# Attention's value products issued once per pair of heads, the first head's one step later

## The reference

```
sc = einsum('bhqd,bhkd->bhqk', qi, k) * scale      # + decay terms for the fox heads
sc = where(kpos <= qpos, sc, -inf)
p  = softmax(sc, axis=-1)
o  = einsum('bhqk,bhkd->bhqd', p, v)               # the value product
```

## Time and profile before

| | us |
|---|---|
| median of 3 runs | 959.61 |
| lowest and highest of them | 958.34 and 964.16 |
| the profiled execution, its own time | 958.37 |
| its span in the trace | 956.5 |

### The profile page before, as it was taken

The page is one execution under the profiler, slowest core; times in us unless marked ns, Lnnn a source line. Parts: engine busy times, 40 slices in busy tenths (PEclk is TensorE's granted clock), DMA queues, the critical chain, the costliest instruction groups (busy, mean ns, idle before and its releaser), DMA issues.

```text
span 956.5 us, 13462 instructions
## 1 busy us (share of the span) xinstructions
PE 927.1 (97%) x5645; PEld 815.0 (85%) x5645; DVE 680.6 (71%) x784; ACT 497.0 (52%) x629; POOL 56.4 (6%) x79
## 2 busy tenths in 40 slices
PE   8999999999999999989999999999899999999997
PEld 7999878888888799976688888887899898888886
DVE  4976895897896865566758975668677866566664
ACT  5646854544636565666544545555354544444442
POOL 2025002000000000010010000000000000000000
PEclk9999999999999999999999999999999999999999
DMA  9743278899895462223579976655555455665531
GB/s 299 233 134 133 93 265 287 282 349 333 283 308 179 132 221 72 89 89 132 167 283 341 323 270 201 217 179 174 173 183 182 150 183 191 194 199 176 183 126 45
DMA packets 122756, 192.54 MB, mean 201 GB/s; under 512 B 6630, under 2 KB 103176, under 8 KB 119496
## 3 DMA queue, kind: packets, MB, share of 16 engines
q1 hardware_dynamic: 116496, 157.00, 50.2%
q0 software_dynamic: 5824, 33.90, 9.7%
q10 hardware_dynamic: 376, 0.78, 0.2%
HBM read 190.60 MB, written 1.06 MB: 200 GB/s over the span
## 4 chain that ended last, share of the span: by engine, by line
PE 71%; DVE 8%; ACT 4%; issue 2%; DVEq 0%
PE PS L663 19%; PE PS L664 10%; PE PS L615 9%; PE PS L617 9%; PE PS L616 9%; PE PS L608 3%; PE PS L610 3%; PE PS L609 3%; DVE lo L1698 3%; ACT hi L1230 1%; DVE stats L1784 1%; PE PS L736 1%; DVE r L1777 1%; DVE x_tok L1797 1%; ACT hid L1559 1%
## 5 line engine op out<-in xcount | busy, mean ns | idle before, releaser
L1698 DVE TENSOR_TENSOR lo<-raw,hi 128x2048 fp32r<-128x2048 f32 (+1 forms) x147 | 329.5, 2264 | 94.3 <-ACT hi L1230 94.2
L663 PE MATMUL PS<-x_both,hi 128*128 128x512 f32 x848 | 297.0, 393 | 0.0
L1230 ACT ACTIVATE hi<-raw 128x2048 fp32r<-128x2048 f32 (+1 forms) x147 | 271.7, 1885 | 9.1 <-DMA raw<-even_w_in 5.1
L664 PE MATMUL PS<-x_both,lo 128*128 128x256 f32 x848 | 237.5, 280 | 0.0
L663 PEld LDWEIGHTS PS<-x_both,hi 128*128 128x128 f32 x848 | 159.0, 187 | 35.7
L664 PEld LDWEIGHTS PS<-x_both,lo 128*128 128x128 f32 x848 | 159.9, 189 | 1.3
L615 PE MATMUL PS<-hi,hid_hi 128*128 128x512 f32 x352 | 139.3, 396 | 0.5 <-DVE hid_lo L1997 0.5
L617 PE MATMUL PS<-hi,hid_lo 128*128 128x512 f32 x352 | 138.9, 394 | 0.0
L616 PE MATMUL PS<-lo,hid_hi 128*128 128x512 f32 x352 | 138.8, 394 | 0.0
L608 PE MATMUL PS<-x_both,hi 128*128 128x256 f32 (+1 forms) x472 | 135.0, 286 | 3.0 <-DVE lo L1698 1.7
L609 PE MATMUL PS<-x_both,hi 128*128 128x256 f32 (+1 forms) x472 | 133.3, 282 | 0.0
(11 more groups left out here) (302 smaller groups left out, 1002.7 us busy)
## 6 DMA issues: line engine op xcount, KB each, us to landing
raw<-ffn_w_gate SPq DMA_DIRECT2D x22, 1024.0 KB, 7.8
raw<-ffn_w_up SPq DMA_DIRECT2D x22, 1024.0 KB, 6.3
raw<-ffn_w_down SPq DMA_DIRECT2D x22, 1024.0 KB, 5.1
raw<-mlp_w_in SPq DMA_DIRECT2D x16, 1024.0 KB, 5.3
raw<-mlp_w_out SPq DMA_DIRECT2D x16, 1024.0 KB, 5.0
sq<-ada_w POOLq DMA_DIRECT2D x12, 1024.0 KB, 7.1
r<-ada_w POOLq DMA_DIRECT2D x12, 1024.0 KB, 5.9
raw<-sc_w_in SPq DMA_DIRECT2D x12, 1024.0 KB, 5.2
```

The costliest lines, as they stand in the source:

```text
L663: pe.matmul(PS[:, bank + m, :], wh, x_both[:, :, k, :], start=k == 0, stop=False, skip_group_check=True)
L664: last = pe.matmul(PS[:, bank + m, 0:S], wl, x_hi[:, k, :], start=False, stop=k == KT - 1, skip_group_check=True)
L1230: act.activation(split_view("hi", c), split_view("raw", c), ACT.Copy).then_inc(hi_split, 1)
L1698: dve.tensor_tensor(split_view("lo", c), split_view("raw", c), split_view("hi", c).bitcast(F32), ALU.subtract).then_inc(lo_split, 1)
```

## The change

Only PE's program changes. `attend` now takes a pair of heads. It is called at even steps from 4 on, so the odd head's value product stays at its step, and the even head's moves from the odd step before to this one. The four products of the pair are written head by head for the first key block and then head by head for the second. The wait for `prob_t_ready` now asks for both heads, the wait for `o_lo` stands ahead of the pair, and `attended` still counts once for each head.

```diff
-            def attend(a):
-                pe.wait_ge(sem("prob_t_ready"), a + 1)
-                pair, e = a // 2, a % 2
-                if e == 0 and pair >= 1:
+            def attend(pair):
+                pe.wait_ge(sem("prob_t_ready"), 2 * pair + 2)
+                if pair >= 1:
                     pe.wait_ge(sem("o_lo"), pair)
-                if a in (0, FOX_H):
-                    pe.wait_ge(sem("odd_evac"), 18 if a else 2)
-                v, h = (v_tok, a) if a < FOX_H else (vm_tok, a - FOX_H)
-                pt = prob_t[:, a % 2, :]
-                pe.matmul(PS[64 * e:64 * e + 64, 3, 0:S], v[:, 0, h * 64:h * 64 + 64], pt[:, 0:S], start=True, stop=False,
-                          skip_group_check=True)
-                pe.matmul(PS[64 * e:64 * e + 64, 3, P:S], v[:, 1, h * 64:h * 64 + 64], pt[:, S:384], start=False, stop=True,
-                          skip_group_check=True).then_inc(sem("attended"), 1)
+                if pair in (0, FOX_H // 2):
+                    pe.wait_ge(sem("odd_evac"), 18 if pair else 2)
+                v, h = (v_tok, 2 * pair) if pair < FOX_H // 2 else (vm_tok, 2 * pair - FOX_H)
+                for j, qs, ks in ((0, slice(0, S), slice(0, S)), (1, slice(P, S), slice(S, 384))):
+                    for e in range(2):
+                        last = pe.matmul(PS[64 * e:64 * e + 64, 3, qs], v[:, j, (h + e) * 64:(h + e) * 64 + 64], prob_t[:, e, ks],
+                                         start=j == 0, stop=j == 1, skip_group_check=True)
+                        if j:
+                            last.then_inc(sem("attended"), 1)
...
-                if a >= 3:
-                    attend(a - 3)
+                if a >= 4 and a % 2 == 0:
+                    attend(a // 2 - 2)
```

## The result

The median after is 962.53 us of 10 executions (960.26 to 968.98), against 960.25 us (957.22 to 965.17) for the kernel before on the same chip: ratio 1.0039, 95% interval 1.0020 to 1.0058. By the ratio the change costs some 3.7 us (1.9 to 5.6); the two medians differ by 2.3. The forecast was 959.1, the range ended at 961.5, and the time lies above it, though within the 1% that was called no change.

The account below looks back on a forecast made before the run. PE bounds the whole kernel (97% busy), but ACT and DVE often bound the changed stretch. A gain of 1.5 us, less 0.3 and 0.65 given back, left -0.55 us: median 959.61 becomes 959.1, range 956.8 to 961.5.

Parts of the forecast that it names:

- Steps 3 and 4: Early attention: PE waits for DVE anyway up to 411.81, so the PE time saved there buys nothing.
- step 5: Attention, where head 2's product and its 1.63 us wait leave: `uq` 1 starts 3.07 us sooner, shift only -1.5 us.
- the wait before step 8: PE idle ahead of that step's scores, which wait for ACT: grows from 1.08 to 3.3 us.
- What a pair costs: Two heads' value products on PE: 0.92 us against 1.78 apart; seven pairs can gain 0.86 each, 6.0 us of PE.
- Rival 2: The two heads of a pair don't overlap on PE in this order: +1.4 us, 961.0; chance 0.05.
- term of 0.64: Extra us per pair if its heads don't overlap, counted three times on the chain: -0.55 + 3 x 0.64 = +1.4.
- Rival 3: ACT and DVE have more slack in steps 5 to 15, so PE's savings pass through: about 957.0 us; chance 0.10.
- steps 10 and 16: ACT's copies of heads 8 and 14 wait for the pair behind the transposes: 0.3 and 0.65 us given back.
- The shift is -1.2 us from there: From ACT's copy of head 8, starting at 442.6 instead of 443.83, carried through the later steps.
- rival 1: PE's clock falls in the longer wait, half speed for 3 us takes 1.5: +0.65 us, 960.3; chance 0.33.
- the shift stays: After the attention, PE's long feed-forward work has nothing of the change in it, so -0.55 us reaches the end.
- steps 16 to 18: End of the attention, no cover left: the copy waits for the pair, 0.65 given back, leaving -0.55 us.

Follow-up runs that it names:

- before_again: The kernel before, unchanged, run again for a second trace: 958.49 us, ratio 0.9995.
- four_buffers_warm: The changed kernel with four buffers for transposed probabilities instead of two, plus idle PE products where PE waits: 957.04 us, ratio 0.9983.
- pairs_warm_short: The changed kernel with idle PE products, each group sized a little under the PE wait it fills: 958.89 us, ratio 0.9994.
- warm_tail: The changed kernel with idle PE products only at the end of the attention: 959.55 us, ratio 1.0006.
- tail_single: The changed kernel with one pair undone, heads 12 and 13 issued apart as before: 958.51 us, ratio 1.0002.
- pairs_again: The changed kernel, unchanged, run again for a second trace: 964.18 us, ratio 1.0053.

## Why the prediction was wrong

**The steps before step 8: right against the profiled execution.** Steps 3 and 4 bought nothing; step 5 gave 1.58 for 1.5; the wait before step 8 was 3.29 for 3.3. Against `before_again` step 5 gives 0.16 (its mask of step 6 comes 3.75 after that of step 5, after's 3.59): see the base below.

**What a pair costs: right.** Six of after's eight pairs read 0.87 us for eight records, for 0.90, and the two that lie in a fall read 1.55. Rival 2 (no overlap) and its +1.4 are out. (Its term of 0.64 is not worked out; from the prediction's own rows it would be 2 x 0.80 + 0.09 - 0.92 = 0.77.) Rival 3 is out for this kernel, since A with the clock held came out at the forecast's shift; but what it says of slack is in part true: once the copy's wait is gone (`four_buffers_warm`), 2.13 of shift reaches L615, not 1.5. This also decides the weighing of the Trainium skill (TensorE: Matmul & The Clock Gate, The mechanism): under strict program order, read pass by pass as the prediction reads it, the pair would have cost 0.12 more, and the trace disagrees in the changed order too.

**Where ACT's wait for the pair leaves the chain at steps 10 and 16: right** with the clock held, -1.35, -0.51 and -0.55 in `pairs_warm_short`. What the wait takes was sized too low, 0.95 against 1.6; it didn't show because the transposes stood further ahead than the -1.5 that it was taken from.

**Failed: "The shift is -1.2 us from there", and with it rival 1's price.** Rival 1 had the mechanism and the first place: the clock fell behind the 3.3 us wait, the copy of head 8 shifted -0.23, near rival 1's 0. It was given 0.33 and should have been the forecast: the row that spoke against a fall has 1.78 us of idle time, and the earlier trace rows a fall behind 1.53 and 1.63, both shorter than the wait of 3.3 that was worked out.

**Failed: "the shift stays" after step 18.** Neither forecast nor rival asked what the price at the end does to PE's own waits. PE waits 1.41, 0.72, 0.58 and 0.97 us there in after (0.28, none, 0.55 and 0.93 in the earlier trace rows). The 1.41 is the place that head 12's product left; the 0.72 is the copy that starts later, and with four buffers it is gone. In both traces of after the clock falls there and stays at 0.50 for 10.2 us. Against `pairs_warm_short`, which met the forecast in these steps, this is 1.05 us within steps 16 to 18, from the copy of head 14 (1.1 late, the price of step 8's fall) to L615 (2.16 late), and 2.52 in the output product, a place that isn't in the change. That this place carries most of the loss is what `warm_tail` and `tail_single` show: with it filled or undone alone the ratio is 1.0006 and 1.0002, with intervals that hold 1.

**Failed: the base.** -0.55 was taken against an execution that held a fall of 1.45 us at step 5. The view stood in the prediction, as an argument for rival 1, and the sum didn't use it: the part of the -1.5 us that came from PE at half speed belongs to that execution, not to the order. Against an execution without it the order costs +0.9 us with the clock held. With both falls the traces give 51.20 - 48.15 = 3.05 in A and 2.52 in B, 5.6 us, or 4.1 against the profiled execution before. The medians differ by 2.3 in the first comparison and 4.9 in `pairs_again`'s: not every execution of after has both falls, and not every one of before is without.

**The range** ended at 961.5 since rival 1 was sized as one fall that returns what had been won. The runs show a price that isn't bounded so: in after it went on into 5.9 us of output product that the change doesn't touch.

**What stays open.** Why a fall comes in one execution and not in the next: at step 5 of before in one trace of two, and in after, where 6 of 22 executions have a mean clock of 0.992 or more. At an equal mean clock of 0.996 after's four executions (960.26 to 961.76) lie about 2.2 us above the kernel before's mean of 958.98, of which the order explains 0.9. The other 1.3 may be where the low windows lie, which the mean doesn't tell, or chance: the kernel before's 25 executions at 0.996 run from 957.28 to 964.15. No run tested it. That the wait itself, and not something else in the changed steps, makes the clock fall is shown only through idle products that fill it; both go together.

## What to carry to other kernels

Where an engine isn't the bound in a stretch, time saved on it becomes a wait, and on TensorE a longer wait can lower the granted clock of the dense work behind it: work out the new waits first, and price them by the work that follows too, past the end of the stretch that was changed. Read the granted clock of the profiled execution by windows before taking any shift from it, and take one trace more of the kernel before when it holds a fall. A product issued in pairs asks for buffers for two pairs: with four buffers instead of two, and idle products in the waits, this order is the fastest version measured (0.9977, 0.9966 to 0.9988, measured once).

## What the runs showed of the hardware

The clock stayed at 0.50 through 5.9 us of output product in which PE was never idle, after the sparse steps before it; full clock came back only behind it. The Trainium skill (TensorE: Matmul & The Clock Gate, What's actually happening) puts the penalty of the ramp, the slow stretch ahead of full clock, at under 1% of a typical kernel's span. The falls here come in the middle of the kernel, but their price is of that size too: A and B together are 4.7 us longer in after than in `pairs_warm_short`, in 960. For this change it is nearly the whole effect.

Over 140 executions of the kernel before, beside the runs of the four rounds, the time goes with the mean granted clock: 957.16 us at 0.998 (mean of 18 executions), 958.98 at 0.996 (25), 960.09 at 0.994 (17), 961.18 at 0.992 (7), 962.06 at 0.990 (7); a straight line through all 140 gives 4.6 us for 0.01. A hundredth of PE's time is 9.6 us, so by this estimate about half of what the clock takes reaches the end. The line accounts for 44% of the variance of the times: the mean clock is less than half of this kernel's scatter, and the rest lies elsewhere, as in the 6.9 us ahead of step 5 in `before_again`. After's executions lie mostly below 0.992 (16 of 22), the kernel before's in 13 of 140.
